# Second scan of a two-block model: where VectorE sums the state, and where GpSimd and ScalarE do the attention branch's work

## The reference

```
state = state * w_t + (state @ a_t) outer b_t + v_t outer k_t
y_t = state @ r_t
out = x + gate * (merged(sigmoid(g_a) * br_a, sigmoid(g_b) * br_b) @ w_o)
br_b = (y_b * silu(z_b)) @ w_pb
```

## Time and profile before

| what | value |
|---|---|
| median of three runs | 2587.17 us |
| profiled execution, its own time | 2581.97 us |
| its span | 2580.2 us |
| TensorE busy | 2475.6 us, 96% |
| VectorE busy | 1347.9 us, 52% |
| GpSimd busy | 985.9 us, 38% |
| ScalarE busy | 852.0 us, 33% |
| mean granted clock of TensorE | 0.985 |

### The profile page before, as it was taken

One profiled execution on the slowest core, in us unless ns is written; L12 is line 12 of the kernel. 1 busy time (PEld: TensorE's weight loads), 2 busy tenths in 40 slices (PEclk: granted clock), 3 DMA queues, 4 the chain that ended last, 5 costly groups with the idle time before them and its releaser, 6 DMA issues. The chain is left out here.

```text
span 2580.2 us, 41164 instructions
## 1 busy us (share of the span) xinstructions
PE 2475.6 (96%) x17425; PEld 2023.1 (78%) x17425; DVE 1347.9 (52%) x2063; ACT 852.0 (33%) x1402; POOL 985.9 (38%) x524
## 2 busy tenths in 40 slices
PE   7998999999999999999999899999998998988998
PEld 6887788888888888888877568778785777887786
DVE  6112643253252221222675589999994664556842
ACT  4314563321120110123443464544515542123231
POOL 3222434443343342344573226546623102231774
PEclk9999999999999999999999999999998998899999
DMA  3112312122222111112234204234233002102423
GB/s 139 48 43 90 123 41 106 49 86 86 86 84 81 63 46 49 50 49 83 81 102 161 65 27 132 85 98 141 78 106 127 22 12 92 37 5 96 160 74 114
DMA packets 82085, 207.68 MB, mean 80 GB/s; under 512 B 8392, under 2 KB 21744, under 8 KB 81904
## 3 DMA queue, kind: packets, MB, share of 16 engines
q1 hardware_dynamic: 74992, 192.48, 22.9%
q10 hardware_dynamic: 6912, 12.59, 1.4%
HBM read 170.81 MB, written 35.27 MB: 80 GB/s over the span
## 5 line engine op out<-in xcount | busy, mean ns | idle before, releaser
L332 PE MATMUL ps<-region_rounded,weights_hi_by_slot 128*128 128x512 f32 x2432 | 962.5, 396 | 19.8 <-DVE region_rounded L640 14.2
L334 PE MATMUL ps<-region_rounded,weights_lo_in_place 128*128 128x512 f32 x2432 | 948.5, 390 | 0.0
L333 PE MATMUL ps<-region_rounded,weights_hi_by_slot 128*128 128x512 f32 x2432 | 948.4, 390 | 0.0
L326 POOL TENSOR_TENSOR weights_lo_in_place<-wbuf,weights_hi_by_slot 128x1024 fp32r<-128x1024 f32 x194 | 485.6, 2506 | 668.0 <-ACT weights_hi_by_slot L322 667.7
L332 PEld LDWEIGHTS ps<-region_rounded,weights_hi_by_slot 128*128 128x128 f32 x2432 | 458.0, 188 | 123.3 <-issue 26.9
L334 PEld LDWEIGHTS ps<-region_rounded,weights_lo_in_place 128*128 128x128 f32 x2432 | 457.6, 188 | 96.3
L333 PEld LDWEIGHTS ps<-region_rounded,weights_hi_by_slot 128*128 128x128 f32 x2432 | 458.1, 188 | 95.6 <-issue 3.9
L322 ACT CAST weights_hi_by_slot<-wbuf 128x1024 fp32r<-128x1024 f32 x194 | 201.7, 1043 | 373.0 <-DMA wbuf<-w_mlp 215.9
L2175 DVE MAX8 gcols<-region 128x8 f32<-128x384 f32 (+5 forms) x192 | 171.7, 894 | 6.6
L2177 DVE MATCH_REPLACE8 region<-gcols,region 128x384 f32<-128x384 f32 (+5 forms) x192 | 168.2, 876 | 0.0
L1462 POOL TENSOR_TENSOR region_rounded<-region,region_rounded 128x512 fp32r<-128x512 f32 x64 | 83.0, 1297 | 215.3 <-DVE region_rounded L1615 215.3
(11 more groups left out here) (359 smaller groups left out, 3489.0 us busy)
## 6 DMA issues: line engine op xcount, KB each, us to landing
wbuf<-w_mlp SPq DMA_DIRECT2D x64, 512.0 KB, 3.6
wbuf<-w_hn SPq DMA_DIRECT2D x37, 512.0 KB, 4.2
wbuf<-w_in SPq DMA_DIRECT2D x25, 512.0 KB, 3.7
region<-xT SPq DMA_DIRECT2D x24, 512.0 KB, 7.0
xtra<-w_ada SPq DMA_DIRECT2D x32, 384.0 KB, 4.2
scratch_hn_out<-tmp ACTq DMA_DIRECT2D x48, 256.0 KB, 4.1
region<-scratch_hn_out SPq DMA_DIRECT2D x24, 512.0 KB, 8.2
wbuf<-w_att SPq DMA_DIRECT2D x20, 512.0 KB, 3.7
```

The source lines that it names most:

```text
L326: self.nc.gpsimd.tensor_tensor(self.m.lo4[:, n % SLOTS, :], self.m.raw4[:, n % SLOTS, :], self.m.hi4[:, n % SLOTS, :].bitcast(F32), ALU.su ...
L332: nc.tensor.matmul(out, m.hi4[:, s, w], m.rounded(hi + k, half(hf)), start=(k == 0), stop=False)
L333: nc.tensor.matmul(out, m.hi4[:, s, w], m.rounded(lo + k, half(hf)), start=False, stop=False)
L334: return nc.tensor.matmul(out, m.lo4[:, s, w], m.rounded(hi + k, half(hf)), start=False, stop=(k == KT - 1))
```

## The change

Three edits, in the order of the diff. GpSimd, from iteration 1 on, waits for `s_scaled` to count 2i ahead of its pass over the region chunk. ScalarE's rounding in iterations 0 to 3 stands behind the copies of u, and not ahead of them. VectorE's `level` takes a chunk, and calls `add_state_and_output` for it behind the level's two masks; level 1 gets chunk 2i-2 and level 3 chunk 2i-1, and the calls between `first_inverse` and level 1, and between levels 2 and 3, are gone. The last two chunks, behind the loop, stay as they were.

```diff
                 k = i % 4
+                if i:
+                    pool.wait_ge(s_scaled, 2 * i)
                 if i < 4:
...
                     nc.scalar.copy(wt[:, i % 2, par, :, :], by_pair(m.ps[:, B + par, 0:256])).then_inc(wt_copied, 1)
+                for h in range(2):
+                    act.wait_ge(uv_ready, 2 * i + h + 1)
+                    nc.scalar.copy(uv[:, i % 2, 256 * h:256 * h + 256], m.ps[:, rows_bank(i, h), 0:256]).then_inc(uv_copied, 1)
                 if i < 4:
                     act.wait_ge(attn_gated, i + 1)
                     nc.scalar.copy(m.rounded(YB_HI + i), m.chunk(YB + i)).then_inc(attn_hi, 1)
-                for h in range(2):
-                    act.wait_ge(uv_ready, 2 * i + h + 1)
-                    nc.scalar.copy(uv[:, i % 2, 256 * h:256 * h + 256], m.ps[:, rows_bank(i, h), 0:256]).then_inc(uv_copied, 1)
...
-            def level(i, l):
+            def level(i, l, c=None):
+
                 mask_level(i, l, 0)
                 mask_level(i, l, 1)
+                if c is not None:
+                    add_state_and_output(c)
                 if l > 1:
                     grow_cols(i, l - 1, 1)
...
                 first_inverse(i)
-                if i:
-                    add_state_and_output(2 * i - 2)
                 if i == 0:
                     dve.wait_ge(y1_cleared, 3)
-                level(i, 1)
+                level(i, 1, 2 * i - 2 if i else None)
                 if i:
                     add_u(2 * i - 1)
                 level(i, 2)
-                if i:
-                    add_state_and_output(2 * i - 1)
-                for l in range(3, LEVELS):
+                level(i, 3, 2 * i - 1 if i else None)
+                for l in range(4, LEVELS):
                     level(i, l)
```

## The result

| | before | changed |
|---|---|---|
| median | 2584.65 us (2579.85 to 2591.28, 12 runs) | 2592.8 us (2588.98 to 2595.48, 12 runs) |
| ratio | | 1.003, 95% interval 1.0021 to 1.0039 |
| profiled execution | 2581.97 us | 2593.58 us |
| its span, mean granted clock | 2580.2 us, 0.985 | 2590.9 us, 0.977 |

The change made the kernel slower by 0.3%: 5.4 to 10.1 us by the interval, where the forecast's sum was 2.9 us. The runs of before were repeated, and their median came out 2.5 us lower than the one that I started from; the difference is what counts. In the profiled executions it is 11.6 us.

What follows compares the result with a forecast made beforehand. TensorE's order of work was taken as the path, so edits count by its waits. The terms -3.9+7.9+0-1.1 = +2.9 us took the median 2587.17 to 2590.1, given as 2590; range 2579.5 to 2597 for 8 in 10.

Steps and rivals of the forecast that it cites:

- Edit 1: Second scan, level 1: chunk 2i-2's state moved behind the masks; gain 3.9 us, bounds 0 and 5.2.
- T0: Start of TensorE's products that level 1's masks are to mask; forecast steps at level 1 count from it.
- d: Duration of VectorE's scale of chunk 2i-2's state before; forecast gain d-0.48 an iteration, 3.9 us over seven.
- edit 2: Level 3: chunk 2i-1's state moved behind the masks delays growth and TensorE by 1.13 us an iteration; loss 7.9 us.
- the lower bound: At level 1, a gain of 0: TensorE's supply of instructions takes what the earlier state read gains.
- edit 3: GpSimd's pass waits for `s_scaled` 2i; claimed 0, with the transfer burst's hole the same elsewhere, from -1.6 to +1.6 us.
- Rival 3: New 1.13 us idle at level 3 lets the clock fall, up to 3.5 us an iteration; above 2594.9 us, chance 0.15.
- the 186.4 us: First mask of iteration 1 to end of iteration 7, before; forecast wrong if under 182 or over 194 us.
- the likeliest case: The forecast's own sum holding, 2586 to 2594.9 us; chance 0.52.
- Edit 4: ScalarE's rounding behind the copies of u, iterations 0 to 3: TensorE's chunk loads wait less; gain 1.1 us, from 0.
- Rivals 1 and 2: Supply hides level 3's state, 2582.2 us, chance 0.22; with it, less level 1 idle keeps clock up, 2575 us, 0.11.

Runs made afterwards that it cites:

- l1_only: The kernel before with only chunk 2i-2's state moved behind level 1's masks: 2586.37 us, ratio 1.0008.
- pool_only: The kernel before with only GpSimd's pass made to wait for `s_scaled`: 2584.34 us, ratio 1.0002.
- l3_only: The kernel before with only chunk 2i-1's state moved behind level 3's masks: 2596.81 us, ratio 1.0043.
- l3_fill4: The changed kernel with 4 useless TensorE products filling the hole at level 3 in iterations 1 to 7: 2585.72 us, ratio 1.0004.
- act_only: The kernel before with only ScalarE's rounding moved behind the copies of u: 2583.55 us, measured once.
- l3_undone: The changed kernel with chunk 2i-1's state put back between levels 2 and 3: 2583.27 us, ratio 0.999.
- spread: l3_undone with SP's eight transfers of the gate chunks issued apart, one per iteration: 2582.53 us, ratio 0.9988.

## Why the prediction was right in its range and short in its sum

**Edit 1, right to 0.03 us in its steps.** Forecast: second mask T0+0.99, state add T0+1.20, scale T0+1.65, TensorE's products T0+1.05, state read T0+2.10. In iteration 4 after, with T0 = 2267.13: 2268.10 (the pair's end less one mask, T0+0.97), T0+1.18, T0+1.62, T0+1.05, T0+2.10. The scale takes 0.42 us. From `first_inverse` to level 3's first mask, iteration 5 takes 9.19 us before and 8.26 in l1_only (0.93 gained, forecast d-0.48 = 0.87). The changed kernel has 8.18 there; the other 0.08 are edit 2's, whose three instructions no longer stand ahead of that mask. Over all seven iterations it is 3.0 us (64.2 less 61.2), forecast 3.9 (its own terms, 7.2-7*0.48, give 3.8). Holes on TensorE that no engine ends take a part, such as 0.44 us ahead of L2686's loads at 2273.95 in iteration 4: the lower bound's mechanism, at a quarter of its size. What I overlooked: pool_only has 8.27 us in the same stretch of iteration 5. So edit 3 alone brings all of the gain; moving the state as well brings level 1's masks forward by 0.13 us and level 3's not at all.

**Edit 2, right, to 0.01 us an iteration.** The path grew by 1.12 us from level 1's first mask to level 4's (l3_only above), forecast 1.13. Between the masks of levels 3 and 4 alone it is 1.20 us (2.20 before, 3.40 in l3_fill4), because level 3's mask comes 0.08 us earlier. Of the 0.25 us that I gave the state's old place at most, 0.08 were real. Seven times 1.12 are the forecast's 7.9 us.

**Rival 3 is the term that was mis-sized.** I gave 0.15 to "the new idle lets the clock fall in the iterations that now keep 1.00", against it one row, in which TensorE idled a stretch long and the clock held. It fell in all four. The clean row against it, iteration 6 before, was one stretch of one iteration; the stretch 2190 to 2192, in which PE was busy for 1.33 of 2 us and behind which the clock did fall within some 3 us, counted as much, and I had both in front of me.

Its price: the changed kernel and l3_fill4 differ in the filling products alone. Iterations 4 to 7 take 113.4 us in the one, at 0.81 to 0.83, and 102.5 us in the other, at 1.00. That is 2.7 us for each, where I had said up to 3.5. In the medians, 7.5 us lie between the two (8.15 and 0.66 over their own before), with mean clocks of 0.978 and 0.9865. Before, at 0.983, lies between them. At this rate, 0.9 us per 0.001, the low clock costs some 4.6 of the 8.15 us against before, which leaves 3.5 for the path; at the rate of 1.5 us per 0.001 in the last section it costs 7.7, which leaves 0.4. Both are estimates; the forecast's 2.9 lies within them.

So the sum of the path was sound, and a low clock that the sum left at nothing came on top. My test said "wrong if the 186.4 us become more than 194": they became 198.1, and by that test the forecast failed. Rival 3, as I had written it, would have put the time above 2594.9. That it came to stand inside the likeliest case's own range is luck, and the starting point helped: that range reaches 7.8 us above the median that I started from, and the change cost 8.15 us (7.8 by the ratio) against a before whose median came out 2.5 us lower.

**Edit 3, right.** GpSimd's pass began at 2276.66 and its next masking at 2289.72, with 10.7 us idle between. No instruction beside it grew. The burst of transfers moved behind it at no loss or gain that shows. With the early burst, iteration 3 takes 28.30 us (before), 31.20 (act_only), 31.29 (l1_only) and 33.94 (l3_only); with the late one 28.41 (changed), 28.60 (l3_undone), 30.19 (pool_only) and 31.41 (l3_fill4). Its hole is there in both: 1.08 us with no releaser at 2257.82, behind the changed kernel's burst of 2250.70, which is the "same hole elsewhere" of the forecast.

**Edit 4, right in its waits:** 1.1 us of them, gone in act_only. No time of so many runs tells 1 us.

**Rivals 1 and 2, refuted.** TensorE's idle time ahead of the seventeenth load at level 3 grew from 0.11 to 1.30 us, so supply did not hide it. The clock did not rise with less idle at level 1: in l1_only it averages 0.981 over eleven runs, against 0.983.

**What stays open.** Edit 1 or 3 takes some 4 us from the path up to level 1's masks in the profiles, and the ratios of l1_only, pool_only and l3_undone stand for +2, 0 and -2.5 us against before, with intervals of some 5 us. In all three profiles the stretch behind level 4 is longer than before (66.7 to 70.1 against 64.2) at a lower clock. Whether the time gained at level 1 is given back there by rule or by chance, these runs, with one profile each, don't settle. Nor do they say why the clock fell in some iterations of l3_undone, pool_only and spread that have no long hole at level 3. In iteration 0 (some 30 us at clock 0.66 to 0.72 everywhere) a hole of 3.05 us stays in spread, where four of the transfers at the scan's start have moved away; other transfers still run beside it.

## What to carry to other kernels

An engine's small instructions that sit in a gap of their own cost next to nothing (here 0.08 us); moved behind another pair of instructions, they cost their whole length if what follows the pair releases TensorE (here 1.13 us). Look for the next releaser before moving, not only for the one that gets earlier. Where two edits remove the same wait (here a move on VectorE and a wait on GpSimd), count it once. And a new hole of a microsecond on TensorE should be priced with the clock that may fall behind it: here 2.7 us in each iteration where it fell, twice the hole.

## What the runs showed of the hardware

**Time follows the clock from run to run.** Over 79 runs of the kernel before, the mean granted clock lies between 0.980 and 0.988, and the time falls by 1.5 us for each 0.001 of it (correlation -0.82). I take that for an upper end of the clock's price, since holes cost time themselves. The changed kernel's twelve runs have 0.976 to 0.980: none is as high as the mean of before, 0.983.

**A scale with both operands in SBUF waits for GpSimd's whole pass.** A VectorE multiply with both operands in SBUF stretched from 0.42 to as much as 1.50 us, ending 0.28 to 0.29 us after GpSimd's pass in all seven iterations of before; adds with one operand in PSUM, beside the same pass, kept 0.41 us. The Trainium skill (SBUF — State Buffer, Who interferes with whom) says that such an instruction contends with a GpSimd instruction that reads SBUF. By that rule ordering the pass behind the scale is enough, and the trace of pool_only agrees: 0.43 us.

**Filling TensorE raises its clock, and pays only in the long hole.** Four useless products in a hole of 1.3 us, in seven iterations, gave 7 us back; one in each of four holes of some 0.3 us per iteration raised the mean clock by 0.003 and gave nothing.

**Beside a burst of transfers the next packet of instructions comes late.** Beside four transfers of 512 KB issued together, the next instruction packet on q8 started 5.9 to 8.9 us behind the last in eleven traces, in place of some 4 us, and TensorE stood idle nearby for 1.1 to 4.4 us with no releaser.
